# Second block of layers as one stream of half-width tiles, its first half beside the last expert gathers

## What is computed

```python
# end of the first block: 16384 experts, 8 heads, 16 experts per head and token
idx = top16(cand); g = softmax(top)
a = gelu(einsum('tpkd,td->tpk', u[idx], t))
x = x + gt2 * einsum('tpk,tpkd->td', g * a, v[idx])
x = rms_norm(x, norm_f)
# second block
for i in range(2):
    if i == 1: k, v = split(rmsnorm(x, kv_norm) @ w_kv)
    h = rmsnorm(x, norm_mix[i])
    if i == 0: y_tok = short_conv(h @ a_w_in)          # 3 taps over time
    else:      y_tok = window_attention(h @ b_w_q, k, v)  # 12 heads, window 128
    y_mem = memory_attention(q_mem, mem_k[i], mem_v[i])   # 4 heads, 256 keys
    x = x + concat(y_tok, y_mem) @ w_out
    h = rmsnorm(x, norm_ffn[i])
    x = x + (silu(h @ w_gate[i]) * (h @ w_up[i])) @ w_down[i]   # width 2816
return rmsnorm(x, final_norm)
```

## Time and profile before

| what | us |
|---|---|
| median of three runs | 3521.12 (3512.99 to 3540.35) |
| the profiled execution, its own time | 3531.02 |
| its span, first to last instruction | 3529.2 |
| PE busy in the span | 2780.4 (79%) |
| DVE / ACT / POOL busy | 1678.9 / 729.1 / 1116.0 |
| DMA, whole span | 707.11 MB, mean 200 GB/s |
| mean granted clock of TensorE | 0.929 of full |

### The profile page before, as it was taken

How to read it: one execution, slowest core, us unless ns; L and a number is a source line. 1 busy time by engine, 2 the same in 40 slices (tenths; PEclk the granted TensorE clock), 3 DMA queues, 4 the chain that set the end, 5 groups by cost and what they waited for, 6 DMA issues and landing times. The chain is left out here.

```text
span 3529.2 us, 35080 instructions
## 1 busy us (share of the span) xinstructions
PE 2780.4 (79%) x12300; PEld 1593.7 (45%) x12300; DVE 1678.9 (48%) x3574; ACT 729.1 (21%) x1291; POOL 1116.0 (32%) x1028
## 2 busy tenths in 40 slices
PE   7887877980266666667666799698899989889998
PEld 4766765450011111111111122476688845568886
DVE  3223773688855555556566400433433325443334
ACT  4443653210000000000000000223322215432222
POOL 0000000356677777777777767000000000000000
PEclk8998988995699999999999999898999999899999
DMA  6222101577799999999999999220333220123331
GB/s 246 94 93 86 43 20 75 201 282 283 275 362 367 354 359 366 362 359 384 356 358 356 409 389 398 85 76 27 117 96 98 82 84 1 54 78 95 96 96 54
DMA packets 190519, 707.11 MB, mean 200 GB/s; under 512 B 21280, under 2 KB 22560, under 8 KB 186528
## 3 DMA queue, kind: packets, MB, share of 16 engines
q0 software_dynamic: 147456, 536.94, 40.4%
q1 hardware_dynamic: 42912, 168.23, 14.4%
HBM read 702.98 MB, written 2.10 MB: 200 GB/s over the span
## 5 line engine op out<-in xcount | busy, mean ns | idle before, releaser
L1590 PE MATMUL ps<-pe_ring,pe_spot 128*32 128x512 f32 x2048 | 911.2, 614 | 348.5 <-DMA pe_ring<-in_v,pe_vidx 346.4
L1535 POOL DMA_INDIRECT pe_ring<-in_u,pe_idx x512 | 565.0, 1103 | 920.7 <-DVE pe_idxf L1789 656.0
L1803 DVE CUSTOM_DVE_ANT_0 pe_ring<-pe_ring,pe_htok 128x1024 f32<-128x1024 f32 x512 | 617.9, 1226 | 487.6 <-DMA pe_ring<-in_u,pe_idx 485.7
L1590 PEld LDWEIGHTS ps<-pe_ring,pe_spot 128*32 128x32 f32 x2048 | 184.9, 111 | 1065.4 <-DMA pe_ring<-in_v,pe_vidx 728.5
L1545 POOL DMA_INDIRECT pe_ring<-in_v,pe_vidx x512 | 550.8, 1076 | 168.1 <-issue 123.7
L203 PE MATMUL ps<-ff_r_hi,ff_w_hi 128*128 128x512 f32 x704 | 275.7, 392 | 31.5 <-DVE ff_w_lo L175 31.5
L204 PE MATMUL ps<-ff_r_lo,ff_w_hi 128*128 128x512 f32 x704 | 275.1, 391 | 0.0
L205 PE MATMUL ps<-ff_r_hi,ff_w_lo 128*128 128x512 f32 x704 | 274.9, 390 | 0.0
L175 DVE TENSOR_TENSOR ff_w_lo<-wring,ff_w_hi 128x1024 fp32r<-128x1024 f32 x136 | 166.3, 1225 | 171.5 <-ACT ff_w_hi L171 165.8
L171 ACT ACTIVATE ff_w_hi<-wring 128x1024 fp32r<-128x1024 f32 x136 | 142.6, 1051 | 155.0 <-PE ps L205 155.0
L203 PEld LDWEIGHTS ps<-ff_r_hi,ff_w_hi 128*128 128x128 f32 x704 | 132.9, 189 | 61.0 <-DVE ff_w_lo L175 33.2
(11 more groups left out here) (368 smaller groups left out, 3782.5 us busy)
## 6 DMA issues: line engine op xcount, KB each, us to landing
wring<-in_gate SPq DMA_DIRECT2D x44, 512.0 KB, 3.6
wring<-in_up SPq DMA_DIRECT2D x44, 512.0 KB, 3.6
wring<-in_w_in SPq DMA_DIRECT2D x32, 512.0 KB, 4.1
wring<-in_down SPq DMA_DIRECT2D x32, 512.0 KB, 3.5
wring<-in_a_in SPq DMA_DIRECT2D x20, 512.0 KB, 3.6
xT<-in_w_mod SPq DMA_DIRECT2D x8, 1024.0 KB, 4.8
hT<-in_w_mod SPq DMA_DIRECT2D x8, 1024.0 KB, 4.9
wring<-in_wq SPq DMA_DIRECT2D x16, 512.0 KB, 5.3
```

The costliest lines, as they stand in the source:

```text
L1535: pool.indirect_dma_start(ring[:, n % RU, :], None, io["u"], bass.IndirectOffsetOnAxis(idx[:, t, j:j + 1], 0)).then_inc(land_u[n % RU], 16)
L1590: mm = pe.matmul(ps[PER * grp:PER * grp + PER, 2 * (t % 2) + half, :], spot[:, grp, i * PER:(i + 1) * PER], ring[:, RU + n % RV, half * 51 ...
L1803: dve.tensor_tensor_reduce(ring[:, n % RU, :], ring[:, n % RU, :], htok[:, t, :], 1.0, 0.0, ALU.mult, ALU.add, dots[:, t % 2, j:j + 1]).th ...
```

## The change

The first block up to the routing is as before. From there on the program is one block for all engines.

- Half width: the second block runs twice, half(0, ...) for tokens 0 to 255 and half(1, ...) for 256 to 511. Each of its 184 products per half (PRODUCTS) has 256 columns. Every weight tile is loaded, and split into high and low part, once per half, so twice in all. The convolution's last two columns are carried over (carry), k and v of the window are kept.
- All products are three-pass, those that were single-pass too. They go through 3 PSUM slots (BANKS) and 5 raw weight slots (RAW), the low part written over the raw tile.
- The norm is not applied before a product: PE multiplies x times gain, unnormalised, and the factor rstd is multiplied in where the product leaves PSUM (scaled). The 8 square chunks of a norm are made while the projection before it runs (chunk_out), its root by Ln and Exp (root).
- half(0) runs beside the gathers of the last part: tile 2 from its 65th u gather on, and tile 3. Its products and attention units are ticks, 204 of them; the 448 gathers left are spread evenly over them, 2.2 per tick (Beside). At each tick DVE first does the dots due (dots_beside), PE the v sums due (sums_beside), ACT the placing of weights (weights_beside). A v sum is due 6 gathers after its own issue or later (sum_at).
- POOL's order: u of tile 0; v0 and u1 in turn; v1 with the first 64 u of tile 2, two to one; 64 u of tile 2 and 8 of tile 3 alone; v2 and u3 in turn; v3 alone. The rings have 7 slots each instead of 8. In the phase of v1 DVE also does all choosing for tile 3, twice two units in a row.
- pe_spot holds a quarter of a tile's weights at a time, placed in 4 rounds.
- Attention works on units of two heads and one query tile: 4 memory units in the first layer of a half, 4 memory and 12 window units in the second. PE does score(u+1), turn(u), weigh_v(u-1); DVE logits(u+1), probs(u). Both score matmuls go into banks 4 and 5, of which there is one pair.
- The output is stored transposed, straight from DVE's result (the host turns it back); the turning at the end is gone.

```diff
@@ class Attention, rms_block calls, memory_attention, residual_block, feed_forward blocks: gone @@
-        RU, RV = 8, 8
+    RU, RV = 7, 7
...
+    HT = T // 2
+    RAW, BANKS = 5, 3
...
+    EARLY = HK // 2
+    AHEAD, STEP = 8, 3
+    U3_AT = HK - EARLY
+    V2_AT = U3_AT + AHEAD
+    V3_AT = U3_AT + 2 * HK
+    GATHERS = V3_AT + HK
+    def sum_at(t, j):
+        return V3_AT + 4 * STEP + j if t == 3 else min(V2_AT + 2 * j, V3_AT - P + j) + 2 * STEP
...
+    class Beside:
+        def until(self, at):
+            while self.next is not None and self.next <= at:
+                self.next = next(self.steps, None)
+        def __call__(self):
+            self.tick += 1
+            self.until(self.tick * GATHERS / TICKS)
...
-                for t in range(TT + 1):
-                    for j in range(P):
-                        if t:
-                            gather_v(t - 1, j)
-                        if t < TT:
-                            gather_u(t, j)
+            for j in range(P):
+                gather_u(0, j)
+            for j in range(P):
+                gather_v(0, j)
+                gather_u(1, j)
+            for j in range(P):
+                gather_v(1, j)
+                if j % 2:
+                    gather_u(2, j // 2)
+            for j in range(EARLY, P):
+                gather_u(2, j)
+            for j in range(AHEAD):
+                gather_u(3, j)
+            for j in range(P):
+                gather_v(2, j)
+                if j + AHEAD < P:
+                    gather_u(3, j + AHEAD)
+            for j in range(P):
+                gather_v(3, j)
...
+            def product(n, hi, lo, nk=KC, chunk_in=None):
+                pe.wait_ge(st_lo, n + 1)
+                if n >= BANKS:
+                    pe.wait_ge(st_free[n % BANKS], n // BANKS)
+                for k in range(nk):
+                    pe.matmul(slot(n), parts_hi[:, n % SPLIT, k, :], hi[:, k, :], start=k == 0, stop=False)
+                    pe.matmul(slot(n), parts_hi[:, n % SPLIT, k, :], lo[:, k, :], start=False, stop=False)
+                    mm = pe.matmul(slot(n), w_lo[:, n % RAW, k, :], hi[:, k, :], start=False, stop=k == nk - 1)
+                mm.then_inc(st_used, 1)
...
+                score(0)
+                for u in range(len(units) + 1):
+                    if u < len(units):
+                        beside()
+                        if u + 1 < len(units):
+                            score(u + 1)
+                        turn(u)
+                    if u:
+                        weigh_v(u - 1)
...
+            def scaled(p, n, dst, by=None):
+                r = rstd[:, p * HT:(p + 1) * HT]
+                dve.wait_ge(st_used, n + 1)
+                dve.tensor_tensor(dst, slot(n), r, ALU.mult).then_inc(st_free[n % BANKS], 1)
...
+                for u in range(len(units) + 4):
+                    if u >= 4 and u % 2 == 0 and u - 3 < len(units):
+                        out_lo(u - 3)
+                    if u < len(units):
+                        beside()
+                        logits(u)
+                    if 0 < u <= len(units):
+                        probs(u - 1)
...
+                for f0, count in FF_GROUPS:
+                    for f in range(f0, f0 + count):
+                        beside()
+                        scaled(p, n, g_ff[:, f % 2, :])
+                        split_lo(n + SPLIT)
+                        if f > f0:
+                            hidden_lo(f - 1, f0)
+                        beside()
+                        scaled(p, n + 1, up_ff[:, f % 2, :])
+                        dve.wait_ge(silu_done, (2 * p + layer) * FT + f + 1)
+                        dve.tensor_tensor(hid_ff[:, f % 2, :], silu_ff[:, f % 2, :], up_ff[:, f % 2, :], ALU.mult).then_inc(hid_done, 1)
+                        split_lo(n + 1 + SPLIT)
+                        n += 2
...
+            for j in range(EARLY):
+                if j == 16:
+                    add_sum(0, 0)
+                    choose(2, 2)
+                if j == 32:
+                    add_sum(0, 1)
+                    choose(2, 3)
+                    choose(3, 0)
+                if j == 47:
+                    token_indices(2)
+                if j == 48:
+                    choose(3, 1)
+                    choose(3, 2)
+                if j == 56:
+                    choose(3, 3)
+                dot(2, j)
+            token_indices(3)
+            add_sum(1, 0)
+            add_sum(1, 1)
+            beside = Beside(dots_beside())
+            half(0, beside)
+            beside.rest()
+            half(1, Beside())
```

1785 lines of the change are left out of this document (971 added, 814 removed).

## The result

| | before | changed |
|---|---|---|
| median of 11 runs each, one chip | 3521.12 (3512.99 to 3541.45) | 3562.59 (3549.18 to 3581.86) |
| ratio, 95% interval | | 1.011 (1.0085 to 1.0134) |
| profiled execution, span | 3529.2 | 3564.4 |
| PE busy | 2780.4 | 2735.7 |
| DVE / ACT / POOL busy | 1678.9 / 729.1 / 1116.0 | 1938.4 / 977.6 / 1161.2 |

The changed kernel is 1.1% slower on the chip of this comparison. On another chip, further down, the same pair comes out 1.3% the other way, so whether this change gains or loses is not settled by one chip; what it gains and what it pays can be read stage by stage.

A forecast was written before the change was run, and what follows sets the result against it. It took gathers to bound the gather stage and PE the second block. First product 1629, first half 1163, seam to 2814, second half 714 and 9 at the end gave span 3537, 3529 on the median's scale; range 3390 to 3660.

The forecast's parts named there:

- the seam: Between the halves: closing tile 3, norm and first chunk with nothing beside, 9.3 + 12 us, to 2814.
- In all +25: Gather stage before the first half: choices delaying POOL with 7 ring slots add 25 us, to 1598.
- PE's work in a half, 544: Each half: 518 us of matmuls at 0.120, 9 of waits at product starts, 17 of ones products.
- the rival with the issue gap: Products: the skill page's 109 ns per 256-column matmul holds, 93 us less, 3436; chance 0.03.
- Waits at product starts, 0.05 x 184 = 9: Each half: PE waits 0.05 us at each of 184 product starts, 9 us in all.
- Attention, 146 + 18 per half: Each half: serial units at half clock, 8 x 7.1 + 12 x 7.45 us, plus 18 for filling, emptying and clock.
- DVE at the start, +61 and +10: First half's first 28 products: DVE sets 144 us instead of 83, plus 10 for a falling clock.
- Transfers, +25: First half: gathers and tiles at the lower 366 GB/s add 18 us in layer one's feed-forward, 7 elsewhere.
- Waits add up: First half: half of the 256 v sums keep a 0.93 us wait for rows, +119 us, 3648; chance 0.18.
- Full clock in attention: Attention stays at full clock and DVE's start is cheaper: 119 us less, 3410; chance 0.29.
- DVE slowing POOL: Gathers beside DVE's work take 1.99 instead of 0.94 us on POOL: +70 us, 3600; chance 0.08.
- No overlap: First half: rings starve and it runs at the gathers' pace plus its own, 3800; chance 0.02.

The follow-up runs named there:

- e7_all: Changed kernel with weights placed before later exps, split_hi first, last hidden chunk's low part first and weighing before turning: 3455.29 us, 0.9425 of the kernel before.
- e1_act_order: Changed kernel with ACT placing each quarter of tile 1's weights before exps of later choices: 3588.29 us, 0.9799 of the kernel before.
- e9_all_spread_filler: e7_all plus v1-phase choices made singly after each ten dots and 6 unused turnings in second-half attention waits: 3420.19 us, 0.9348 of the kernel before.
- e2_split_first: Changed kernel with ACT rounding the next weight tile (split_hi) before steps that wait for DVE: 3519.05 us, 0.9582 of the kernel before.
- e3_lo_first: Changed kernel with DVE making a group's last hidden chunk's low part before the next weight tile's: 3591.66 us, 0.9829 of the kernel before.
- e4_weigh_early: Changed kernel with PE doing weigh_v(u-1) before turn(u) in attention: 3581.74 us, 0.9798 of the kernel before.
- e6_filler: Changed kernel with 8 unread turnings of the unit matrix in PE's wait, second-half attention: one run, 3600.84 us, 0.9843 of the kernel before.
- e5_serial: Changed kernel with all remaining dots, v sums and placings done before the first half, nothing beside it: one run, 3903.12 us, beside 3658.33 before.

## Why the prediction was right or wrong

It forecast 3529 as the likeliest time, no change within 1%, and 3390 to 3660 as the range; 3562.59 lies in the range, on the slower side, 1.1% above before. Of the three outcomes it had given faster the most, 0.41. That the total is so near is in good part luck, because errors of both signs met: +65 at the start, -63 in the first half, -2 in the seam, +28 in the second half. And on the slower chips the same kernel took 3615.12.

*Start, 1629 forecast, 1693.8 measured.* The failed step is "In all +25". It counted what choices cost POOL through the rings, and took ACT's placing of weights as free. Its program order put three placings behind choices that DVE makes later, 74.2 us of waits. That was in view: the code's order of exps and place_weights, with DVE's choices beside it. The 65 us lie in three places. The first v gather comes at 940.40, 8 us later than the 932.2 taken. The 256 gathers of v0/u1 take 384.8 us, to 1325.22, where the step had 366 and 10. Here the rate of 1.43 was the slip, for the kernel before had spent 376.1 on the same 256: the mean over the whole stage hides that this part is slower. From there to the first product are 368.6 us where the step had some 320, and the runs show two layers of that: ACT's order is 27 to 35 us (e7_all, e1_act_order), and the doubled choices, which then stand in the wait's place with 17.45 and 11.00 us, another 19 (e9_all_spread_filler against e7_all; the forecast gave them 24). What 7 slots in place of 8 cost, no run shows apart.

*PE's work in a half, 544.* Right in the price: 482 matmuls in 57.9 us of the convolution of the second half, 0.120 each, and the rival with the issue gap falls. (The Trainium skill, TensorE: Matmul & The Clock Gate, Back-to-back issue gap, gives that gap for a matmul by itself and says that in a stream with operand loads both set the spacing, so by its own words the rival's 109 ns was not for these products.) Wrong in "Waits at product starts, 0.05 x 184 = 9": the second half takes 751 - 114 (attention) - 11 (from the last ones product, 3553, to the end) = 626 us where the step had 550. It treated DVE and ACT as free in the second half because they are half idle. They are idle in good part because they wait for each other. e2_split_first takes 77 us out of this half and so shows the cause; e3_lo_first rules out the order of the last two steps as the main part.

*Attention, 146 + 18 per half.* The clock was called rightly (0.52 to 0.57). The unit was not: 5.64 us where the step had 7.45. It nearly doubled the row's 1.15 and 1.05 us for two heads. But the score's operands of two heads lie in rows 0 to 63 and 64 to 127: four score records of 64 rows now take 1.22 us, as two did in the earlier trace rows, and eight weighings, whose outputs lie so too, 1.12 where four took 1.11. The Trainium skill (TensorE: Matmul & The Clock Gate, Part 3: Packing small matmuls — row/col tiling) says that tiles at different positions of the array run side by side; the trace agrees with 1.22 for both. Scores 2.0 to 1.2 and weighing 1.9 to 1.1 are 1.6 of the 1.8 us. (The parts listed for a window unit add up to 7.3 and not 7.45, and turning was taken as 0.8 where it took 1.05.) 26 + 88 = 114 us for both blocks, 50 less than forecast. That it is a serial chain is shown by e4_weigh_early, that the clock lengthens it by e6_filler.

*DVE at the start, +61 and +10.* Right in size: the first score comes at 1798.8, 105 us on, for 20 products, 5.25 us each where the step has 144/28 = 5.1. In that stretch DVE is busy 93 us and PE 70, so DVE is the fuller of the two but not "near full".

*Transfers, +25.* Wrong, they cost nothing: in the feed-forward with the gathers beside it PE is busy 352 of 360 us at 339 GB/s. "I take the lower rate" was the failed choice. In the whole first half PE waits little for rows, by its waits from 1700 to 2794 us:

```profile
PE ps L1665 <- DMA pe_ring<-in_v,pe_vidx: 1.7, 4, 0.5
```

The two terms that were too high, attention (50, if the first half saves what the second does) and transfers (25), make 75, where the first half came out 63 shorter; the 12 between them aren't assigned.

*The rivals.* "Waits add up" falls by that row (1.7 us where it had 119). It carried 0.17 of the 0.35 given to slower, so that chance rested for the most part on a mechanism that isn't there: the loss is at the start and in the second half, which no rival named. Full clock in attention falls (0.52 to 0.57). DVE slowing POOL: not tried alone; the first feed-forward shows no loss for it to explain, and a v gather takes 1.12 us of POOL on average where it took 1.08. No overlap falls by e5_serial, where the overlap is worth 270 to 290 us.

## What to carry to other kernels

When an engine serves two streams, write down for each of its waits what stands behind it: a copy that others wait for must not queue behind a step whose input is made later, and a step that needs nothing (rounding the next weight tile) goes ahead of one that waits. Two engines that are each half idle can still be the bound, if they wait for each other in turn; compare their period (here 6.85 us) with that of the busy engine (5.8), rather than their busy shares. After one wait of this kind is removed, look for the next in the same place before adding up the gain. And where the total is noisy, compare the stage that an edit touches, and check that a stage it doesn't touch has kept its length.

## What was not expected of the hardware

- The speed of indirect gathers differed between two chips, each profiled once: 1.42 and 1.57 us each for the same kernel, which makes its span 123 us longer, while its second block takes 1306 us with PE busy 1198.65 us on the slower chip and as long on the first:

```profile
2223.00:3529.00 1306.00, 1198.61 (x5020) 906.35 (x5020) 517.59 (x929) 387.59 (x678) 0.00 (x0) 0.94 0.24 76
```

- Gathers also spread on one chip: the 256 of v0/u1, the same code, took 398.3 to 424.3 us in four executions on one chip.
- Short waits cost twice. Behind waits of 4.07 and 3.23 us the granted clock was 0.56 for 4.5 us, and 50 us of the feed-forward around two such waits ran at a mean of 0.93; in e2_split_first, where those waits fall from 39.3 to 5.5 us in all, a stretch as long had 1.00.
- Matmuls that compute nothing, put into waits of 2.33 us, kept the clock at its higher level and shortened the unit around them by 1.43 us.
